# Dilated attention: bias, scale and maximum of the scores in one VectorE instruction, on negated scores

## What is computed

```python
scores = jnp.einsum('bnqhd,bnkhd->bnhqk', qb, kb) * (Dh ** -0.5)
scores = scores - slopes[:, None, None] * dist
scores = jnp.where(valid, scores, MASK_VALUE)
lse = jax.nn.logsumexp(scores, axis=-1)
p = jnp.exp(scores - lse[..., None])
o = jnp.einsum('bnhqk,bnkhd->bnqhd', p, vb)
# three dilations (1, 4, 16), mixed by the softmax of their lse
wts = jax.nn.softmax(jnp.stack(lses, 0), axis=0)
out = jnp.einsum('gbsh,gbshd->bshd', wts, jnp.stack(outs, 0))
```

## Time and profile before

| | us |
|---|---|
| median of 3 runs | 3551.85 |
| lowest, highest | 3551.03, 3553.32 |
| profiled execution, its own time | 3553.55 |
| its span, first to last instruction | 3551.7 |
| TensorE busy | 3348.9 (94%) |
| VectorE busy | 2114.8 (60%) |
| GpSimd busy | 1525.5 (43%) |
| ScalarE busy | 962.1 (27%) |
| mean granted TensorE clock | 0.969 of full speed |

### The profile page before, as it was taken

One profiled execution on the slowest core, in us unless ns is written; L12 is line 12 of the kernel. 1 busy time (PEld: TensorE's weight loads), 2 busy tenths in 40 slices (PEclk: granted clock), 3 DMA queues, 4 the chain that ended last, 5 costly groups with the idle time before them and its releaser, 6 DMA issues.

```text
span 3551.7 us, 44576 instructions
## 1 busy us (share of the span) xinstructions
PE 3348.9 (94%) x16088; PEld 2549.3 (72%) x16088; DVE 2114.8 (60%) x3524; ACT 962.1 (27%) x2171; POOL 1525.5 (43%) x1486
## 2 busy tenths in 40 slices
PE   8979999999999999999999978899999978899998
PEld 5666555555555967888888756688888855678887
DVE  7578746544532096556646668488764776645554
ACT  2066210001120064211122264222203245332211
POOL 1044322222321024444455457466544547645554
PEclk9999999999999999999999988999999998999999
DMA  7300223333321100354422100244443200022222
GB/s 251 130 1 2 101 95 119 108 120 116 118 70 57 48 7 31 109 170 157 165 94 89 58 12 11 72 149 150 165 141 101 89 22 16 10 83 87 89 87 80
DMA packets 91097, 317.68 MB, mean 89 GB/s; under 512 B 10816, under 2 KB 13152, under 8 KB 90880
## 3 DMA queue, kind: packets, MB, share of 16 engines
q1 hardware_dynamic: 64224, 218.34, 19.1%
q10 hardware_dynamic: 24768, 90.19, 6.9%
q0 software_dynamic: 1888, 6.29, 0.6%
HBM read 312.68 MB, written 2.10 MB: 89 GB/s over the span
## 4 chain that ended last, share of the span: by engine, by line
PE 84%; DVE 9%; ACT 3%; issue 2%; POOL 1%; DVEq 0%; ACTq 0%; DMA 0%; SPq 0%; POOLq 0%
PE ps L1263 60%; PE ps L612 7%; PE ps L623 3%; PE ps L1265 2%; PE ps L1220 1%; PE ps L1187 1%; PE ps L942 1%; PE ps L956 1%; PE ps L1130 1%; PE ps L978 1%; PE ps L1172 1%; DVE arena L2506 1%; PE ps L1014 1%; DVE arena L2464 1%; PE ps L1202 1%
## 5 line engine op out<-in xcount | busy, mean ns | idle before, releaser
L1263 PE MATMUL ps<-arena 128*128 128x256 f32 (+1 forms) x3744 | 951.5, 408 | 5.9 <-DVE arena L2197 4.9
L1263 PEld LDWEIGHTS ps<-arena 128*128 128x128 f32 x3744 | 711.0, 190 | 210.8 <-issue 7.9
L2636 POOL TENSOR_TENSOR arena<-ring,arena 128x512 f32<-128x512 f32 (+1 forms) x140 | 182.8, 1306 | 842.0 <-PE ps L1263 842.0
L1263 PE MATMUL ps<-arena,ring 128*128 128x256 f32 (+1 forms) x1968 | 506.4, 409 | 3.1 <-ACT arena L1604 3.1
L1263 PEld LDWEIGHTS ps<-arena,ring 128*128 128x128 f32 x1968 | 373.4, 190 | 114.5 <-ACT arena L1604 5.9
L1263 PE MATMUL ps<-hbuf,ring 128*128 128x256 f32 (+1 forms) x1696 | 432.9, 410 | 12.1 <-ACT hbuf L1711 10.9
L1263 PEld LDWEIGHTS ps<-hbuf,ring 128*128 128x128 f32 x1696 | 330.9, 196 | 97.4 <-issue 15.9
L2217 DVE TENSOR_TENSOR arena<-ps,arena 128x256 f32<-128x256 f32 (+1 forms) x180 | 80.0, 444 | 340.8 <-PE ps L1263 235.3
L612 PE MATMUL ps<-hbuf,ring 128*128 128x512 f32 x736 | 269.1, 528 | 4.1 <-ACT hbuf L1711 2.5
L2105 DVE CUSTOM_DVE_ANT_0 aring<-aring,csil,adab 128x1024 f32<-128x1024 f32 x176 | 262.6, 1513 | 1.7
L2222 DVE SCALAR_TENSOR_TENSOR resid<-ps,mod,resid 128x256 f32<-128x256 f32 (+2 forms) x296 | 137.4, 482 | 187.9 <-PE ps L1263 183.3
(11 more groups left out here) (306 smaller groups left out, 5096.2 us busy)
## 6 DMA issues: line engine op xcount, KB each, us to landing
aring<-in_ada ACTq DMA_DIRECT2D x172, 512.0 KB, 4.7
ring<-in_mlp SPq DMA_DIRECT2D x128, 512.0 KB, 3.7
ring<-in_up SPq DMA_DIRECT2D x88, 512.0 KB, 3.3
ring<-in_in SPq DMA_DIRECT2D x56, 512.0 KB, 3.2
ring<-in_down SPq DMA_DIRECT2D x32, 512.0 KB, 3.5
ring<-in_odd_in SPq DMA_DIRECT2D x24, 512.0 KB, 3.2
arena<-in_ada SPq DMA_DIRECT2D x16, 512.0 KB, 13.8
ring<-in_out SPq DMA_DIRECT2D x16, 512.0 KB, 3.3
```

Source lines behind the costliest of these rows:

```text
L1263: return nc.tensor.matmul(ps[:, bank, 0:p.tw], w, x, start=start, stop=stop, skip_group_check=True)
L2636: nc.gpsimd.tensor_tensor(s[3], f0[:, h:2 * h], s[1], ALU.subtract).then_inc(wsum_ready, 1)
```

## The change

It folds line 1969 and line 1977 into one instruction for each block of scores in layers 2 and 3. The bias tables are made 8 times as large (8 is the root of the head's width), the instruction adds the table to the raw scores, multiplies the sum by -1/8, writes it in place, and takes the minimum, which is the negated maximum of the scores. ScalarE's exponential reads the negated scores with a scale of -1. In the other attentions the scale stays 1.

```diff
+RISE = DH ** 0.5
...
-    return dict(cos=cos, sin=sin, win=win, na=na.reshape(P, 3, 256), dist=rel * np.ones((P, 1)), logc=logc * np.ones((P, 1)),
+    return dict(cos=cos, sin=sin, win=win, na=na.reshape(P, 3, 256), dist=rel * np.ones((P, 1)), logc=RISE * logc * np.ones((P, 1)),
...
                     nc.scalar.activation(probs_of(layer, p, hx)[:, 0:key_tiles(pair) * P], pair_slot(p, pair, hx), ACT.Exp,
+                                         scale=-1.0 if pair[0] == "e" else 1.0,
                                          bias=small[:, i % 4:i % 4 + 1], accum_out=small[:, 4 + i % 4:5 + i % 4]).then_inc(pair_probs, 1)
...
-                        chain(nc.vector.scalar_tensor_tensor(out=s, in0=s, scalar=0.125, in1=BIAS[:, 2 * b + hx, at:at + 512],
-                                                             op0=ALU.mult, op1=ALU.add))
+                        nc.vector.tensor_tensor_reduce(s, s, BIAS[:, 2 * b + hx, at:at + 512], -1.0 / RISE, 3e38, ALU.add, ALU.min,
+                                                       small[:, i % 4:i % 4 + 1]).then_inc(pair_maxed, 1)
+                        return
...
-                chain(nc.vector.scalar_tensor_tensor(out=BIAS[:, h, :], in0=DIST, scalar=-SLOPES[h], in1=LOGC,
+                chain(nc.vector.scalar_tensor_tensor(out=BIAS[:, h, :], in0=DIST, scalar=-RISE * SLOPES[h], in1=LOGC,
...
-                nc.gpsimd.tensor_scalar(BIAS[:, h, :], DIST, -SLOPES[h], 1.0, ALU.mult, ALU.mult).then_inc(pool_step, 1)
+                nc.gpsimd.tensor_scalar(BIAS[:, h, :], DIST, -RISE * SLOPES[h], 1.0, ALU.mult, ALU.mult).then_inc(pool_step, 1)
```

## The result

| us | before | after |
|---|---|---|
| median of 5 runs | 3551.85 | 3522.79 |
| lowest, highest | 3550.40, 3553.32 | 3518.68, 3536.23 |
| span of the profiled execution | 3551.7 | 3521.0 |

The medians are 29.1 us apart. The ratio is 0.9929 with an interval of 0.9914 to 0.9943, which is 25 us less, where 13.1 were forecast. With the runs of the experiments there are 68 executions of the kernel before (mean 3548.5 us) and 15 of the one after (mean 3524.7 us), a gain of 24 us. Both kernels spread widely: the one before from 3539.4 to 3557.7 us, the one after from 3517.5 to 3536.6, and the latter in two groups, ten runs up to 3524.2 and five from 3532.3 on.

What follows compares the result with a forecast made beforehand. VectorE's two blocks per pair were taken to bound the attentions of layers 2 and 3. Gains of 2.2, 1.2, 1.2 and 1.95 us made 6.55 a layer, 13.1 in all: 3538.8 us forecast, range 3533 to 3546.

Steps and rivals of the forecast that it cites:

- the block, 0.79 us: VectorE's score block in layers 2 and 3: 0.79 us start to start instead of 1.34, saving 0.55 us.
- shifts and keeps its length: Everything behind the meeting of all engines that ends each attention starts earlier but takes as long: no gain there.
- the clock in the attentions: Range term: shorter TensorE pauses may bring its upper clock level sooner, up to 2 us less a layer.
- loop of latencies for pairs 9 to 11: Scores, both VectorE blocks, exponential, transposes, next TensorE work: 7.43 us per two pairs before, 6.23 after; TensorE then bounds.
- lower bound of 0.61: Shortest block considered, from the bias instruction with the same operands: another 0.18 us less a block, 3 us in all.
- four blocks: Pairs 0 and 1: VectorE's four consecutive blocks before GpSimd's first scaling, 4 x 0.55 = 2.2 us earlier.
- pair 3's path: From pair 3's bias to its second exponential, 2.79 us before: 1.2 us less.
- pair 5 to the scaling: From pair 5's bias to GpSimd's scaling of pair 4, 2.90 us before: 1.2 us less.
- GpSimd's unbroken work: Pairs 4 to 8: GpSimd's scaling and bias tables run without a stop, 9.4 us, which faster VectorE does not shorten: gain 0.
- The tail: From pair 11's TensorE work to the meeting of the engines: shifts as a whole, no further gain.
- half rate: Rival: the fused form on PSUM takes 1.34 us a block or nearly, giving 3550 to 3553 us; chance 0.10.
- fall of TensorE's clock: Rival: in each attention's last eight pairs TensorE's clock falls, each pair costing 2.7 us more; 3571 us at six; chance 0.03.

Runs made afterwards that it cites:

- give_back: Changed kernel's fused instruction, followed by the old reduction, which alone releases the exponential; against the kernel before: 3553.32 us, ratio 1.0018.
- early_release: Fused instruction releases the exponential with its own minimum, then VectorE does a useless 512-column reduction; against the kernel before: 3550.70 us, ratio 1.0007.
- wide_block: Changed kernel plus one small waited-for VectorE copy behind each fused instruction, making a block 0.82 us; against the kernel before: 3535.25 us, ratio 0.9964.

## Why the prediction was wrong

Two steps of it failed. One term was mis-sized (the block, 0.79 us), and one was put at nothing (what follows "shifts and keeps its length"). The second is what puts the time outside the range: the range's terms, 13.1 with 3 for a shorter block and 4 for the clock in the attentions, reach 20.1 us (3531.8, which the prediction wrote as 3533), and the two attentions of the changed kernel's traces gave 18.6 to 20.6.

- **What bounds the kernel there**: right. VectorE's blocks stood in the path, as give_back and early_release show from both sides. The loop of latencies for pairs 9 to 11 was the wrong reason for it: early_release shortens the latency by 0.7 us a block and gains nothing there. It is VectorE's time that is full.
- **One block, after**: the prediction took 0.79 us from start to start, by the earlier trace rows less 512 columns. Measured: 0.62 and 0.65. What was wrong is the 0.12 us between a read of the accumulator and the next instruction. That is not what the instruction costs; it is a wait that the program has there. In `modulate`, line 2098's sum must have arrived (`wait_ge(ada_first, ...)`) before line 2105 may start. Where no such wait stands, the kernel before shows the same form starting together with the read, 13 us ahead of the earlier trace rows:

```profile
61.84 0.08 DVE L2098 DVE_READ_ACCUMULATOR2_ANT mod<- 128x1 f32 x1
61.96 1.28 DVE L2105 CUSTOM_DVE_ANT_0 arena<-arena,csil,adab 128x1024 f32<-128x1024 f32 x1
63.17 0.08 DVE L2105 DVE_READ_ACCUMULATOR2_ANT mod<- 128x1 f32 x1
63.17 1.28 DVE L2098 CUSTOM_DVE_ANT_0 junk<-arena,csil,adab 128x1024 f32<-128x1024 f32 x1
```

In the whole trace the gap is 0.11 to 0.12 us in all 64 places with the wait, and 0.00 in all 86 places where a fused instruction follows line 2105's read without one. The changed blocks have no such wait on VectorE, so the price was to be had before the change. The column price was good (the read starts 0.62 after its instruction, 0.66 forecast). The lower bound of 0.61, from the row with the same operands in PSUM, was the nearer one, and the prediction put it into the range only. A saving of 0.69 in place of 0.55 a block turns the 6.55 us a layer into 8.2 if the sum is scaled by it; the comparison at equal clock gives 8.0.
- **Sum, layer 2**: its steps held with the new block: four blocks 2.8 (4 x 0.69 = 2.76), pair 3's path 2.79 to 1.47 us (1.3), pair 5 to the scaling 2.90 to 1.50 (1.4), GpSimd's unbroken work 9.4 and 9.5 us, pairs 9 to 11 from 11.43 to 9.32 us (9.48 forecast), with TensorE back to back. Two terms had not been in it. Scores(3) ran at the upper level (1.13 us, 1.50 before), which gave 0.4 by the clock. The tail, which was to shift as a whole, gave 0.5, since its transposes no longer wait for ScalarE's copies. wide_block is the check: with the block at 0.82 the kernel gained 12.7 us, though with a higher clock than the sum assumed.
- **"What follows starts at the meeting of all engines, so it shifts and keeps its length"**: wrong by 3.8 and 5.5 us in the profile, and by another 1.65 between layer 3's tables and its first block. By the means it is some 3 to 5 us. The range had no term for it; it only had one for the clock inside the attention. In its place the runs showed stretches of unchanged instructions in two groups of lengths, which go with the time at TensorE's lower level. That the clock is the whole cause is not shown.
- **Rivals**: half rate did not come; 128x512 took 0.71 us. The rule of the Trainium skill (Vector Engine (DVE) Microarchitecture Reference, 7. Points that are easy to get wrong) is for two sources in SBUF. The fused instruction has one in SBUF and one in PSUM, so its 0.71 us does not test the rule, and the prediction's "by it the change would gain nothing" did not follow. The row with both in SBUF, 1.28 us for 1024 columns, does not bear the rule out, if it covers this form. The fall of TensorE's clock with a busier TensorE did not come either; in the attention the clock rose from 0.87 to 0.91 or 1.00. The change does what it says: x48 and x48 in the fused line, against 48 and 48 instructions before.
- VectorE's busy time fell by 18.5 us, not the 26 named. In the two attentions it fell by 12.9 and 11.0. 48 blocks at 0.69 are 33, but the cumulative sums beside GpSimd's tables are longer (the 48 take 34.8 us, 27.4 before), since by the timeline more of them stand beside GpSimd's two-input instruction. The other 5.4 us arose outside the attentions, and their cause is open.

## What to carry to other kernels

An engine that is 60% busy over the span can be the full one in a stretch of it. There each 0.1 us of its step counts once for every tile, and what releases the next engine early counts for little. Before a step is priced by the distance between two rows, look in the program for a wait between them, and look for another place in the trace where the same two rows stand without one. And where TensorE's granted clock changes level, a stretch of unchanged instructions can differ by 3 to 6 us from trace to trace. Compare stretches that start at a meeting of the engines and have the same granted clock, and take several traces, before a gain is put down to the edit.

## What the runs showed of the hardware

- A fused bias, scale and minimum of 128x512 float32, in and out of PSUM, takes 0.71 us, where the bias alone took 0.69. The read of its accumulator takes 0.14 us, and the next VectorE instruction starts with the read (0.00 us between them in the 48 blocks). At 128x1024 from SBUF it is the same; where the program waits for the sum, the next instruction comes 0.12 us after the start of a read of 0.08.
- The attention of the changed kernel takes 56.5 us at a granted clock of 0.91 and 54.5 at 1.00, with the same instructions. Before the change, at 0.87 to 0.92, it took 64.9 to 64.5: TensorE's clock costs little where VectorE is full. The runs of both kernels order by it roughly (3517.5 us at 0.977 and 3536.6 at 0.970; 3539.4 at 0.973 and 3557.7 at 0.968).
